# Low parts of the input weights: made by DVE two tiles ahead for tiles 4 to 33, by GpSimd from tile 34 on

## The reference

```python
h = _rmsnorm(x, g_mix)
qa, ka, va, qb, kb, vb, rb, a1, ga, gb = jnp.split(h @ w_in, SPLIT_POINTS, axis=-1)
oa = _sink_attend(q, band(ka), band(va), bias, sinks)     # 16 heads, window of 128 + own chunk
ob, s_new = _gla(qb, kb, vb, log_a, s0)                   # 4 heads, gated linear attention
m = sigmoid(ga) * oa + sigmoid(gb) * _rmsnorm(ob, g_ob) * silu(rb)
x = x + m @ w_out
x = x + (silu(h2 @ w_gate) * (h2 @ w_up)) @ w_down
```

## Time and profile before

| | |
|---|---|
| median of 3 runs | 904.92 us (904.55 to 907.67) |
| profiled execution | 906.86 us |
| its span, first to last instruction | 905.1 us |
| TensorE busy | 97% of the span |
| DVE, ACT, GpSimd busy | 64%, 46%, 30% |
| mean granted clock of TensorE | 0.998 of 2.4 GHz |

### The profile page before, as it was taken

How to read it: one execution, slowest core, us unless ns; L and a number is a source line. 1 busy time by engine, 2 the same in 40 slices (tenths; PEclk the granted TensorE clock), 3 DMA queues, 4 the chain that set the end, 5 groups by cost and what they waited for, 6 DMA issues and landing times.

```text
span 905.1 us, 17293 instructions
## 1 busy us (share of the span) xinstructions
PE 879.7 (97%) x7077; PEld 850.0 (94%) x7077; DVE 581.2 (64%) x1124; ACT 415.7 (46%) x762; POOL 272.6 (30%) x161
## 2 busy tenths in 40 slices
PE   6999999999999999999999999999999999999998
PEld 5999999999998999898999988999999999999997
DVE  6864656657884445556465889983279853689732
ACT  6633442445445444444435666542155532366421
POOL 2442323232332323323233212235223153222350
PEclk9999999999999999999999999999999999999999
DMA  8331222221422222221117458863288823788322
GB/s 239 111 86 55 82 59 71 59 82 47 116 71 71 54 64 64 56 70 49 48 43 195 108 119 175 184 142 115 62 176 187 163 83 113 157 178 172 93 79 63
DMA packets 154343, 94.17 MB, mean 104 GB/s; under 512 B 5121, under 2 KB 145111, under 8 KB 154263
## 3 DMA queue, kind: packets, MB, share of 16 engines
q1 hardware_dynamic: 139638, 72.74, 28.4%
q0 software_dynamic: 9504, 17.31, 12.2%
q10 hardware_dynamic: 5120, 3.02, 1.2%
HBM read 71.45 MB, written 3.60 MB: 83 GB/s over the span
## 4 chain that ended last, share of the span: by engine, by line
PE 75%; DVE 14%; ACT 4%; DMA 3%; issue 3%; POOL 0%; SPq 0%; DVEq 0%; POOLq 0%
PE G L640 14%; PE G L642 13%; PE G L641 13%; PE G L916 4%; PE G L918 4%; PE G L919 4%; PE X L916 4%; PE X L918 4%; PE X L919 4%; DVE qAT L1663 2%; PE X L833 2%; PE X L817 2%; DMA csum<-csum 2%; PE X L802 2%; DVE rs L1457 1%
## 5 line engine op out<-in xcount | busy, mean ns | idle before, releaser
L640 PE MATMUL G<-h_hi,w_hi 128*128 128x272 f32 x1280 | 382.9, 299 | 5.5 <-DVE rv L1626 2.3
L642 PE MATMUL G<-h_hi,w_lo 128*128 128x272 f32 x1280 | 370.8, 290 | 0.0
L641 PE MATMUL G<-h_lo,w_hi 128*128 128x272 f32 x1280 | 369.3, 289 | 0.0
L582 POOL TENSOR_TENSOR w_lo<-wraw,w_hi 128x1024 fp32r<-128x1024 f32 x84 | 213.9, 2551 | 398.7 <-ACT w_hi L1050 398.6
L640 PEld LDWEIGHTS G<-h_hi,w_hi 128*128 128x128 f32 x1280 | 241.7, 189 | 14.5 <-issue 10.2
L641 PEld LDWEIGHTS G<-h_lo,w_hi 128*128 128x128 f32 x1280 | 241.9, 189 | 0.8
L642 PEld LDWEIGHTS G<-h_hi,w_lo 128*128 128x128 f32 x1280 | 241.5, 189 | 0.0
L1050 ACT ACTIVATE w_hi<-wraw 128x1024 fp32r<-128x1024 f32 (+1 forms) x129 | 134.5, 1045 | 58.7 <-PE G L642 35.2
L1239 ACT ACTIVATE prob<-prob,nm 128x256 f32<-128x256 f32 (+2 forms) x80 | 36.7, 460 | 63.9 <-DVE sd L1695 63.9
L2009 DVE TENSOR_TENSOR rs<-G,rv 128x544 f32<-128x544 f32 x23 | 16.7, 724 | 75.6 <-PE G L642 75.6
L1370 ACT ACTIVATE sq<-sq 128x544 f32<-128x544 f32 x22 | 14.5, 658 | 96.1 <-DVE sq L1896 96.1
(11 more groups left out here) (321 smaller groups left out, 1838.5 us busy)
## 6 DMA issues: line engine op xcount, KB each, us to landing
wraw<-in_w_in_dram SPq DMA_DIRECT2D x52, 512.0 KB
wraw<-in_w_gate_dram SPq DMA_DIRECT2D x22, 512.0 KB
wraw<-in_w_up_dram SPq DMA_DIRECT2D x22, 512.0 KB
csum<-csum POOLq DMA_DIRECT2D x44, 256.0 KB, 4.8
wraw<-in_w_down_dram SPq DMA_DIRECT2D x16, 448.0 KB
wraw<-csum POOLq DMA_DIRECT2D x22, 256.0 KB, 3.5
wraw<-in_w_out_dram SPq DMA_DIRECT2D x8, 512.0 KB
wraw<-in_w_down_dram SPq DMA_DIRECT2D x8, 512.0 KB
```

The source lines that it names most:

```text
L582: pool.tensor_tensor(w_lo[:, slot, :, :], wraw[:, slot, :, :], w_hi[:, slot, :, :].bitcast(F32), ALU.subtract).then_inc(w_split, 1)
L640: pe.matmul(o, w_hi[:, slot, kc, :], b_hi[:, kc, cols], start=(kc == 0), stop=False)
L641: pe.matmul(o, w_hi[:, slot, kc, :], b_lo[:, kc, cols], start=False, stop=False)
L642: mm = pe.matmul(o, w_lo[:, slot, kc, :], b_hi[:, kc, cols], start=False, stop=(kc == last))
```

## The change

The low parts of tiles 4 to 33 move from GpSimd to DVE. DVE makes the low part of tile n + 2 as the first step of iteration n (n = 2 to 31). GpSimd makes those of tiles 1 to 3, then waits until `w_split` is 34 and goes on with tile 34. The subtraction, its operands and the semaphore are the same.

```diff
--- before.py
+++ after.py
@@ -141,6 +141,7 @@
 EARLY = 2
 SOON = 5
 KEYS_OUT = TILE_OF["qA", 2]
+HANDOVER = UNIT0 + 4
 
 
 def gla_tile(h, step):
@@ -612,7 +613,9 @@
                     low_part(n % RING)
 
             low_rank_low_part()
-            lows(range(1, GU0[0]))
+            lows(range(1, RING))
+            pool.wait_ge(w_split, HANDOVER)
+            lows(range(HANDOVER, GU0[0]))
             for g, m in enumerate(FF_GROUPS):
                 q0 = FIRST[g]
                 first_sums(q0)
@@ -1754,8 +1757,18 @@
                     .then_inc(m_lo_ok, 1)
 
 
+            def weight_low_part(m):
+                s = m % RING
+                dve.wait_ge(hi_done, m + 1)
+                if m == RING:
+                    dve.wait_ge(w_split, RING)
+                dve.tensor_tensor(w_lo[:, s, :, :], wraw[:, s, :, :], w_hi[:, s, :, :].bitcast(F32),
+                                  ALU.subtract).then_inc(w_split, 1)
+
             merged = 0
             for n in range(N_IN):
+                if RING <= n + 2 < HANDOVER:
+                    weight_low_part(n + 2)
                 for h in range(HEADS_B - 1):
                     if n == gla_tile(h, 1):
                         gla_states(h)
```

## The result

The changed kernel takes **900.44 us** (median of 20 runs, 899.17 to 904.76), the kernel before, measured beside it, 905.57 (20 runs): ratio **0.9942, 95% interval 0.9933 to 0.9951**. Predicted were 899.9, between 898.3 and 903.8. The profiled execution took 900.75 us for a span of 898.8, 6.3 less than that of before.

A forecast was written before the change was run, and what follows sets the result against it. TensorE, busy 97% of the span, was taken to set the end, so only its waits counted. The steps sum to -3.3 us, with the clock -5.0: from 904.9 to 899.9, range 898.3 to 903.8.

The forecast's parts named there:

- start of tile 5 (first `vB` copy): Start-up: the low part of tile 6 directly ahead of the copy into `vB` makes TensorE 0.5 us later.
- start of tile 6, with that: Second `vB` copy done earlier, TensorE's 1.17 us wait gone; tile 6 starts 0.85 us earlier, the +0.5 included.
- tile 19: `obT` pair no longer held, low part of tile 20 added before `rv`; TensorE starts 0.80 us earlier.
- head 3's mask: Low part of tile 21 stands before `rv`; TensorE waits about 1.1 us at the mask, 0.95 us lost.
- tile 23: The same `obT` pair and `rv` as at tile 19; 0.83 us won.
- tiles 23 to 30: DVE's loop falls from 7.26 to 6.4 us a tile, below TensorE's 7.04; 0.22 at four boundaries, 0.9 us won.
- turn of unit 0: TensorE's turn, after 1.90 us idle before, comes 0.85 us earlier, with about a microsecond left idle.
- clock: Behind unit 0's turn: with about 1.0 us idle no fall to 1.2 GHz is expected, 1.7 us won.
- Rival (c): Long DVE operations come from their operands, not GpSimd; slower, 922, or 906 to 910 in part; chance 0.06.
- Rival (b): Gains eaten on DVE at the heads of iterations, up to 0.5 at each of eight spots; 903 to 905, chance 0.12.
- Rival (d): The change does nothing, since GpSimd was idle enough; 904.9, chance 0.07.
- Rival (a): The low clock stays or was not in the timed runs, so only 3.3 us are won; 901.6, chance 0.30.

The follow-up runs named there:

- e_both: Changed kernel with GpSimd's subtraction put back for tiles 4 to 33, DVE making each low part again behind it; 926.80 us, ratio 1.0229 to the kernel before.
- e_fill: Changed kernel with GpSimd writing zeros twice into each low part's place (tiles 4 to 33) before DVE makes it; 900.84 us, ratio 0.9935 to the kernel before.
- e_waits34: Changed kernel with its low parts moved, within the same iterations, to where DVE waits for another engine; 895.74 us, ratio 0.9883 to the kernel before.
- e_mask: Changed kernel with only the low part of tile 21 moved behind head 3's mask; 899.32 us, ratio 0.9922 to the kernel before.
- e_hand32: Changed kernel with GpSimd taking over at tile 32 in place of 34; 899.82 us, ratio 0.9930 to the kernel before.
- e_hand26: Changed kernel with GpSimd taking over at tile 26 in place of 34; 903.95 us, ratio 0.9973 to the kernel before.
- e_units: Kernel before with only the low parts of tiles 33 to 36 on DVE, behind the maxima of units 1 to 4; 902.64 us, ratio 0.9966.

## Why the prediction was right, point by point

The changes of TensorE's start, of the two profiles. All of after is 0.5 us earlier from the start-up on, because the first inputs came earlier; this is taken off.

| step of the prediction | predicted | measured |
|---|---|---|
| start of tile 5 (first `vB` copy) | +0.5 | 0.0 |
| start of tile 6, with that | -0.85 | -1.30 |
| tile 19 | -0.80 | -1.01 |
| head 3's mask | +0.95 | +0.85 |
| tile 23 | -0.83 | -0.94 |
| tiles 23 to 30 | -0.9 | -1.32 |
| turn of unit 0 | -0.85 | -1.03 |
| sum | -3.3 | -4.75 |
| clock | -1.7 | about -1.4 over many runs |

**The mechanism held**, though one reading was off: a held product does not end with GpSimd's subtraction. In the earlier trace rows it ends at 247.36 + 2.82 = 250.18, 0.58 us behind GpSimd's 249.60; it waits for that end and then does its work. Rival (c), that the long operations come from their operands, is out by e_both and e_fill: the same DVE instruction takes 0.73 us beside GpSimd's fills and 2.84 beside its subtraction. Rival (b), gains eaten at the heads of iterations, showed only at the mask, where the forecast had it (a wait of about 1.1; 1.02 came). Tiles 7 to 18 had no wait. What the additions at the heads cost up to the turn of unit 0 is the 4.2 us that e_waits34 wins back. Rival (d) is out by the earlier trace rows against their answers above. DVE's busy time was forecast near 581 and is 576.4 (its held operations gave back 41 us and not 37), GpSimd's 197 and is 197.7. One sign that the prediction had listed as wrong did come, a clock fall at another place; its share is told below.

**The term that was mis-sized** is the price of the addition, "1.22 from the same shape on DVE". That is the length of a row; what counts for the instruction behind is the step from start to start, 1.13 (51.56 to 52.70, 269.25 to 270.38; 1.14 a tile in e_both; 1.13 in e_mask). That is 0.1 at each place where a low part lies on the path; it explains tile 23 and most of tile 19: from the held pair to `rv` it is 2.53 us (169.37 to 171.90) instead of 3.47 (171.28 to 174.75), 0.94 won where 0.80 was forecast; the other 0.07 of the 1.01 was won inside tile 6. At the start of tile 5 more was off: the step "it wins 1.94" took only the length of the first product of head 0. Counted from the scan's start, `qL` comes 4.08 us later instead of 5.10, so 1.02 were won there and not 0.72, since the held product also began 0.2 later behind the scan. With 1.14 for the second low part only 0.1 is left of the predicted +0.5, and 0.0 was measured.

**Tiles 23 to 30** were sized by one boundary, 0.26 at 265.45, times four. The products into `qAT` now follow each other by 6.96 us (242.03 to 248.99) instead of 7.26, where the forecast had 7.04, and the seven tiles take 49.49 instead of 50.81 us.

**The clock** was half right. The forecast said that with about 1.0 us idle no fall would follow at unit 0, and none did, in either profile of the changed kernel (0.93 us idle in both). But it counted 1.7 us as if every run of before had a fall and none of after would. Rival (a) said that one profile cannot show this, and that was so: four in five against one in four, at 2.0 to 2.3 us each, makes 0.8 x 2.3 - 0.23 x 2.0 = 1.4 us, and in the profiled pair nothing, since a fall came at 540. The Trainium skill (TensorE: Matmul & The Clock Gate, Part 1) says that the moment of a change varies from run to run. The two profiles of the changed kernel show more than that: with 1.77 and 1.75 us idle at the same place, one had the fall and the other none.

**Does the sum meet the time?** Runs without a fall: 904.58 to 899.75, 4.8 us, against 4.75 from the profiles' starts. With the falls, 6.2 us would be expected, and the two series that give it directly have 5.1 (4.4 to 6.1 by its interval) and 5.9; the difference was not traced. That 899.9 came out so near is in part luck, errors that cancel: the sum without the clock was 1.45 too small, the clock's share 0.3 too large, and the base 0.7 too low (905.6 over 20 runs, not 904.9). With these three put right the same sum gives 899.9 - 1.45 + 0.3 + 0.7 = 899.45; measured were 900.44 and 899.96.

**Left open**: the wait for the low part of `C` at 785 us, which is 1.58 in the profile of before and 0.71 in that of after, lies between 0.26 and 1.70 in the profiles of the other kernels. In the profile of after it ends a chain from a transfer (ACT waited 2.81 us for `csum` ahead of 782.88, then made the high part); whether the change has a part in it was not tried.

## What to carry to other kernels

An engine that is busy 30% of the time can still cost time by what it does to its neighbour: look for one operation with two durations (0.73 and 2.83), and for what the other engine reads when it is long. Work that moves onto the faster engine costs its path only where the engine has no wait of its own; put behind the instruction that starts another engine's turn, a low part cost nothing where that wait was longer than its 1.13 us (1.48 at the mask): the same 30 low parts gave 5 us at the heads of the iterations and 11 in DVE's waits. Price an insertion by the step from start to start, and a clock fall by how often it happens over many runs, not by one profile.

## What the hardware showed that was not expected

- Two GpSimd fills of 128 x 1024 float32 (0.95 to 0.98 us each) in the place of its subtraction do not hold DVE's product with two SBUF inputs (0.73 us), where the subtraction holds it to 2.84.
- The holds seem to go both ways: GpSimd's subtraction took 2.94 us at 265.59 in e_hand32, where it began 0.04 us behind a DVE product with two SBUF inputs (265.55, 0.72 us), against 2.39 and 2.40 for the ones before and after it, and 3.22 at 44.11 in the kernel before, where it began during DVE's scan (43.64, 1.50 us). No run tries this direction by itself.
- An instruction with one SBUF tensor can be held as well: the pair of scalings into `bias` at 261.17 in e_hand32 took 1.59 us under GpSimd's subtraction (260.01 + 2.39 = 262.40) and 0.49 free of it. `rv`, which reads the bank `G`, took its usual 0.72 in the same stretch (260.52).
- A DVE row of 1.20 to 1.23 us holds up the next instruction by 1.12 to 1.14 only.
- The same idle stretch of TensorE, 1.75 to 1.77 us, was followed by 3.4 us at 1.2 GHz in four profiles (after, e_fill, e_hand26, e_units) and by none in the other eight; the 1.89 and 1.90 us at unit 0 were followed by one both times. Behind shorter ones no fall was seen, and in e_both none behind 2.80 us at 54.55 and 1.87 at 60.20 either: length alone does not decide.
